# RWKV scans of a two-block model: rows and bonus become a fifth stage, and the order tables of the scan are drawn anew

## The reference, cut to what matters

```python
def rwkv7_scan(r, w, k, v, kk, a):
    def step(state, inp):
        r_t, w_t, k_t, v_t, kk_t, a_t = inp
        sa = jnp.einsum('bhvk,bhk->bhv', state, -kk_t)
        state = (state * w_t[:, :, None, :] + sa[..., None] * (kk_t * a_t)[:, :, None, :]
                 + v_t[..., None] * k_t[:, :, None, :])
        return state, jnp.einsum('bhvk,bhk->bhv', state, r_t)
...
    for d in range(2):      # forward and backward in time
        ...
        o = rwkv7_scan(*ins)
        bonus = jnp.sum(rh * kd * r_k.astype(F32), axis=-1, keepdims=True) * vh
        dir_out.append((group_norm(o, gn_w, gn_b) + bonus.reshape(nB, S, D)) * g.astype(F32))
    y = dir_out[0] + dir_out[1]
    return y.astype(h.dtype) @ w_o
```

## Time and profile before

| | |
|---|---|
| median of 3 runs | 2982.0 us (2981.33 to 2984.5) |
| the profiled execution | 2981.18 us, its span 2979.5 us |
| busy over the span | PE 92%, PEld 73%, DVE 49%, ACT 41%, POOL 14% |
| the scan, from the first products to the end of the last advance | 2077.73 to 2558 us of the span |

### The profile page before, as it was taken

The page is one execution under the profiler, slowest core; times in us unless marked ns, Lnnn a source line. Parts: engine busy times, 40 slices in busy tenths (PEclk is TensorE's granted clock), DMA queues, the critical chain, the costliest instruction groups (busy, mean ns, idle before and its releaser), DMA issues. The chain is left out here.

```text
span 2979.5 us, 56809 instructions
## 1 busy us (share of the span) xinstructions
PE 2738.0 (92%) x24888; PEld 2161.5 (73%) x24888; DVE 1471.0 (49%) x2295; ACT 1214.5 (41%) x2071; POOL 410.2 (14%) x332
## 2 busy tenths in 40 slices
PE   6999999999999999898889999798777877899999
PEld 5877557788878888775578888676666665678887
DVE  2532774743443333526554242985566764453343
ACT  3332564632242222325443232664556654442232
POOL 1001451000000000103100000001444543100000
PEclk9999999999999999999999999899999999899999
DMA  4222002133222222231222222230000001322221
GB/s 160 96 79 85 1 1 92 71 127 113 99 85 99 92 103 95 81 123 67 76 90 99 95 90 99 86 101 31 6 9 8 8 5 36 114 92 100 85 99 71
DMA packets 38821, 228.84 MB, mean 77 GB/s; under 512 B 4352, under 2 KB 8448, under 8 KB 15024
## 3 DMA queue, kind: packets, MB, share of 16 engines
q1 hardware_dynamic: 32576, 201.34, 18.9%
q0 software_dynamic: 6000, 23.87, 2.3%
HBM read 220.93 MB, written 4.26 MB: 76 GB/s over the span
## 5 line engine op out<-in xcount | busy, mean ns | idle before, releaser
L445 DVE TENSOR_TENSOR weights_lo<-ring,weights_hi 128x1024 fp32r<-128x1024 f32 x353 | 435.4, 1236 | 700.6 <-ACT weights_hi L438 700.5
L438 ACT ACTIVATE weights_hi<-ring 128x1024 fp32r<-128x1024 f32 x364 | 382.2, 1053 | 577.7 <-PE bank L575 335.3
L2506 PE MATMUL bank<-scan_low,scan_low 64*64 64x64 f32 x4608 | 106.6, 233 | 53.7 <-DVE scan_low L2910 31.8
L494 PE MATMUL bank<-mlp_h_hi,weights_hi 128*128 128x512 f32 x384 | 151.3, 394 | 2.0 <-DVE mlp_h_lo L790 2.0
L495 PE MATMUL bank<-mlp_h_lo,weights_hi 128*128 128x512 f32 x384 | 151.1, 393 | 0.0
L496 PE MATMUL bank<-mlp_h_hi,weights_lo 128*128 128x512 f32 x384 | 150.7, 392 | 0.0
L494 PE MATMUL bank<-h_hi,weights_hi 128*128 128x512 f32 x384 | 150.1, 391 | 0.0
L573 PE MATMUL bank<-weights_hi,mlp_p_hi 128*128 128x512 f32 x384 | 149.6, 390 | 0.0
L495 PE MATMUL bank<-h_lo,weights_hi 128*128 128x512 f32 x384 | 149.5, 389 | 0.0
L574 PE MATMUL bank<-weights_lo,mlp_p_hi 128*128 128x512 f32 x384 | 149.4, 389 | 0.0
L575 PE MATMUL bank<-weights_hi,mlp_p_lo 128*128 128x512 f32 x384 | 149.4, 389 | 0.0
(11 more groups left out here) (666 smaller groups left out, 6780.3 us busy)
## 6 DMA issues: line engine op xcount, KB each, us to landing
ring<-in_w_m SPq DMA_DIRECT2D x64, 1024.0 KB, 4.5
ring<-in_w_mb SPq DMA_DIRECT2D x24, 1024.0 KB, 4.6
ring<-in_w_fi SPq DMA_DIRECT2D x22, 1024.0 KB, 4.6
ring<-in_w_fo SPq DMA_DIRECT2D x10, 1024.0 KB, 4.8
ring<-in_w_a SPq DMA_DIRECT2D x7, 1024.0 KB, 4.9
attn_bias<-scratch POOLq DMA_DIRECT2D x16, 448.0 KB, 4.6
ring<-in_w_rg SPq DMA_DIRECT2D x5, 1024.0 KB, 4.9
ring<-in_w_v SPq DMA_DIRECT2D x4, 1024.0 KB, 14.4
```

The lines of the kernel that those rows point to most:

```text
L438: act.e.activation(halves(g, s)[0], raw, ACT.Copy).then_inc(*act.up("act_unit_high", ("high", s)))
L445: lane.e.tensor_tensor(lo, raw, hi.bitcast(F32), ALU.subtract).then_inc(*lane.up(f"{lane.name}_unit_low", ("low", s)))
L494: pe.e.matmul(ps[:, :], hi, xh, start=k == 0, stop=False, skip_group_check=True)
L2506: m = pe.e.matmul(out[to], left[rows], right[rows], start=start, stop=stop, skip_group_check=True)
```

## The change

A fifth stage, **rows (r)**, takes `tbk`, `tv`, the bonus and their drains out of the middle, for the same pair as the middle. The middle begins with the products. Steps hold one operation where they held two to four; empty steps and `quanta` are gone; `ORDER` has new strings for all four engines. POOL makes the first level's mask as soon as the first half of DVE's masks is there (`masked_first`), and no longer makes the masks of level 1 directly after each direction's start of the inverse, but after both. The same instructions are issued as before, in another order; the tables of the head of pair 0 (`EARLY`) put its steps at the same places of the phase before.

```diff
-EARLY = 11
+EARLY = {"pe": (0, 1, 1, 1, 2, 3, 3, 3), "act": (1, 1, 2, 3, 5, 8, 8, 12), "dve": (0, 1, 1, 1, 2, 3, 5, 7)}
...
-ORDER = {"pe": "mmmhthathahhmmttamammamahthamattmammamamamamtamamhhamatmtamhtatmhhhtahmamamamththhama",
+ORDER = {"pe": "ramammrahtammammamrmammamtarmamamahhamamamthaamamarmaamammtaaa",
...
-    plan = {"a": (advance, 0), "t": (tail, -1), "h": (head, 2), "m": (middle, 1)}
+    plan = {"a": (advance, 0), "t": (tail, -1), "h": (head, 2), "m": (middle, 1), "r": (rows, 1)}
...
+def pe_rows(g, pe, b):
+
+    R = g.R
     for d in range(2):
 
         banks = [bank(g, pe, ("tbk", b, d, j)) for j in range(2)]
...
+    banks = [bank(g, pe, ("tv", b, j)) for j in range(2)]
...
+    for e in range(2):
+        ps = bank(g, pe, ("bonus", b, e))
...
+def pool_rows(g, pool, b):
+    pool_scaled_eye(g, pool, b, 1)
+    yield
...
+                if e == 0:
+                    dve.mark("masked_first", b, d)
+                yield
...
     for d in range(2):
-        yield
-        if d == 0:
-            pool_scaled_eye(g, pool, b, 1)
-        yield from quanta(2)
         u = slice(8 * d, 8 * d + 8)
-        pool.wait_ge(g.at("masked_products", b, d))
+        pool.wait_ge(g.at("masked_first", b, d))
...
         masked(0, d)
+        yield
         pool.wait_ge(pool.newest)
...
-        masked(1, d)
-    yield from quanta(2)
-    for d in range(2):
-        masked(2, d)
         yield
...
-    for level in range(2, 6):
-        yield
-        for d in range(2) if level < 4 else ():
-            masked(level + 2, d)
-        yield from quanta(2 if level < 5 else 1)
-    yield
+    for level in range(1, 6):
+        for d in range(2):
+            masked(level, d)
+            yield
```

214 lines of the change are left out of this document (94 added, 120 removed).

## The result

The changed kernel takes 2991.02 us (median of 14 runs, 2986.18 to 2996.61), the kernel before 2982.48 in the same batch (14 runs): a ratio of 1.0029, 95% interval 1.0021 to 1.0037. It is 9 us slower where 18 us less was forecast. A difference of 0.001 between two ratios is 3 us. Each ratio has an interval of 0.0008 to 0.0014 to either side, so two ratios must lie 0.001 to 0.002 apart before the difference is clear.

What follows compares the result with a forecast made beforehand. PE, busy 92% of the span, was taken as the bound, with some 10 us idle per full round. Savings of 13 (six full rounds), 4 (fill round) and 1 (round without a head), 18 us, gave 2964 us; range 2947 to 2983.

Steps and rivals of the forecast that it cites:

- y2 to y5: Middle stretch of a full round: the layout gives 25.8 us, including all 1.8 us of stops on code.
- stops on "issue": PE stopping without a semaphore wait, read as 16 KB code blocks arriving; 55.3 us before, to stay near 50.
- the sum of a full round: Products to y2 18.05, y2 to next products 34.0, code stops 1.8: 53.9 us, against 57.3 over all six.
- the opening: Products to y2: 18.05 us instead of 24.85; 4.9 only moved, 1.9 gained by split masks and products first.
- From the end of y5 to the products: End of a round, a DVE chain of 7.0 us behind y5's drain: 8.65 us, where it was 7.15.
- The fill round: First scan round, head and middle alone, 49.01 us before: waits covered by bonus and head matmuls, 4 us less.
- The round without a head: Scan round after the six full ones, 52.17 us before: only y-to-x waits shrink, 1 us less.
- the last advance: End of the scan, a PE and DVE chain over 8 chunks, 35.40 us before: not touched, 0.
- B: Rival: the head's tail, DVE's seven us behind y5, decides; rounds of 58.0 us, 2989 us in all; chance 0.14.
- D: Rival: PE's stall before x0 of the second direction is larger, ACT's copies holding a bank; 2973, within the forecast's 0.50.
- A: Rival: code blocks at 3.5 us decide, y-to-x waits return as stops; only the fill round gains, 2979; chance 0.18.
- C: Rival: stops overlap DVE's lateness and the clock holds; full rounds of 53 us, 2950 in all; chance 0.15.

Runs made afterwards that it cites:

- e9: Changed kernel with four wide matmuls on constants on PE ahead of its wait for POOL before x0 of the second direction: 2987.55 us, ratio 1.0039.
- e2: Changed kernel with the last products step on PE right behind the third and DVE's masks likewise: 2976.33 us, ratio 0.9984.
- e16: Changed kernel with the last products step ahead of kk2 and the variance but behind `tbk` and the advance step, DVE's masks likewise: 2974.50 us, ratio 0.9985.
- e13: Changed kernel with DVE's `kb` ahead of u of chunk 7 and `bonus_in` ahead of the copy of chunk 7: 2983.08 us, ratio 1.0015.
- e14: e2 with DVE's `kb` ahead of u of chunk 7 and `bonus_in` ahead of the copy of chunk 7: 2965.22 us, ratio 0.9956.
- e1: Changed kernel with POOL's last level 5 mask put before its sum of the tail: 2990.03 us, ratio 1.0027.
- e12: e14 with PE's wait for ACT's copies of the output banks behind the first products instead of ahead of them: 2963.18 us, ratio 0.9960.
- e17: e12 with both of DVE's `minus_kk` ahead of `bonus_in`: 2961.10 us, ratio 0.9937.
- e11: e12 with POOL's low part of the tail behind the level 2 masks, and the edit of e1: 2963.06 us, ratio 0.9957.
- e3: Changed kernel with DVE's `bb` ahead of y5's drain, `kb` ahead of u of chunk 7, `bonus_in` ahead of its copy: 2995.53 us, ratio 1.0046.
- e6: e3 with PE's wait for ACT's copies of the output banks behind the first products instead of ahead of them: 2987.79 us, ratio 1.0026.
- e18: e11 with both of DVE's `minus_kk` ahead of `bonus_in`: 2960.03 us, ratio 0.9936.

## Why the prediction was wrong

**What held.** The waits on y's drain were to fall from 31.8 to under 15: 5.2. A stall of 2.5 us on POOL before x0 of the second direction was to appear: 2.39, and eight in all. The products were to wait for `minus_kk` by 1 to 2 us: they begin 0.11 us behind its end, after 2.02 us of idle time. y2 to y5 was to take 25.8 us: 25.9, with some luck. One of its terms, 2.25 us of wait for u of chunk 5, is 0.43 to 0.50 in five full rounds and 1.81 in one. The stops on "issue" were to stay near 50 us and didn't: 40.9 and 2.6 more, of which 7.7 are the waits for `minus_kk`, so some 36 us, where the kernel before had 55.3 and 5.4 more. The Trainium skill's "Runtime: NRT & Kernel Launch", section "Instruction fetch mechanics", calls the cost of a block's edge mostly hidden; with 36 us left the trace still differs, but no result here turned on it.

**The step that failed** is the sum of a full round, 18.05 + 34.0 + 1.8 = 53.9 us. It measured 58.6, with both ends of it laid out too short. A clean round was to take 53 to 55 us; the shortest of the six took 55.6.
- "The last products step has moved behind `tbk`, kk2 and the variance and ends at 8.1; DVE's masks of it (0.41 each, twice) end at 8.9; POOL makes the mask and the start of the second direction (2 x 1.3) until 11.5": 9.65, 11.1 and 13.2 in the round shown. I let the steps of PE follow each other without asking when their banks come free; three waits for DVE's masks, 1.69 us, are not in the layout. (A step has four masks, not two; POOL starts behind the second, so that slip costs it nothing.) Over six rounds this makes x0 1.2 us late.
- "PE does y1, x1 and xt1 with their drains [...], and y2 starts at 18.05": 21.2. Of the 3.1 us, 1.9 lie behind x0. Some 1.0 is the half clock behind the stall (8.3 us from x0 to y2, 7.3 in e9), for which a layout "by hand at the full clock" has no term, and the rest is work of PE that I took too short. So the opening was worth a loss of 1.7 us, not a gain of 1.9: before, it took 24.4, of which 4.9 us only moved, so 19.5 against 21.2. (The 24.85 of the prediction was misread: y2's first records start at 2322.12, so it is 24.4 in that round too, and the gain laid out was 1.5.) e2 and e16 bring it back to 19.2 and 19.3.
- "From the end of y5 to the products this is 8.65 us": 10.0 as the mean of six (9.0 to 10.9). The chain on DVE was named link by link, but with u of chunk 7 and the copy at no wait (1.07 and 0.41) and the two `minus_kk` at 1.37 us (2.35 beside POOL). Moving `kb` gave 4 to 8 us (e13, e14).
- The rounds' mean was to fall by 2.2 us and rose by 1.3: +7.8 us for 13 forecast the other way. The slower clock, which I had said such a round "feels less", was lower in three of them (0.94). My own rows didn't bear out what I made of it: of the rounds before, the one of 58.55 us had 0.97 like the two shortest.

**The fill round** was to get 4 us shorter and got 0.6 (49.01 to 48.43). **The round without a head** was to get 1 shorter and got 1.8 longer; **the last advance**, at a clock of 0.59 for 0.62, got 0.7 longer. 7.8 - 0.6 + 1.8 + 0.7 is the 9.7 us of the scan.

**The rivals.** B, "It decides once the stretch from y5 to the products is over 10.5 us", gave 2989 and had 0.14. The time is near, and one of its reasons holds (long operations slowed beside POOL); but the stretch is 10.0 us as a mean, over 10.5 in two of six rounds only, the sum ahead of the last mask costs nothing (e1), and two thirds of what the layout missed (3.1 of 4.7 us a round) are in the opening, of which B says nothing. Against the kernel before, though, the end grew more (2.7 us a round) than the opening (1.7). D had the right place and nearly the size: "the step comes 1.5 us later and so does all behind it" is what the round shown has (1.55). What held the step was DVE's masks, not ACT's copies, and the stall itself did not grow. A is out, since the stops on "issue" fell where it wanted them to rise by what y's waits lose; C is out by the time.

The order of the changed kernel with two places mended (e12) takes 12 us less than the kernel before. With a third edit, which is no part of the change (e17), it is 18, the forecast's own figure; that is luck. No trace has the 53.9 us of the layout: the shortest mean of six rounds is 54.2 (e11), e12's is 55.1. What is shown is that the new order can be faster than the old one and that two places in it lost that.

**Open.** What the changed kernel would take with the stall filled to the right length; the 1 us a pair for the clock comes from one trace against another. Why moving the wait for the copies gave 6 us beside e3's order (e6), where the products had waited for it (up to 1.07 us behind `minus_kk`), and nothing from e14 to e12, where they had as well (up to 1.06). And where e17's and e18's gain of 6 to 7 us arises.

## What to carry to other kernels

When a layout by hand sums an engine's work in its new order, put down for each step when its output bank is drained and by whom. A step whose bank is late shifts all behind it, and an engine downstream shows it better (POOL idle for 4.52 us) than the one that slid. Ask of each wide operation at the end of a chain what stands between it and the work that it feeds. Where the operation ahead in the queue waits for another engine, putting a wide one before it was worth 4 to 8 us (`kb`); putting another still further ahead, where it waited itself and held up a drain, cost 5 (`bb`). A pass that nobody waits for belongs behind the step that others wait for, where it fills the stall (e16). An edit's sign belongs to the order around it: "products first" gave 13 us in one and took 14 in the other.

## What was not expected of the hardware

The same stall of 2.4 us was followed by a lower clock in six of eight pairs and not in the other two. Two stretches of the changed kernel, each from x0 on, behind a stall of 2.39 and of 2.54 us (columns as in the earlier trace rows):

```profile
2194.06:2199.36 5.30, 5.30 (x204) 5.18 (x206) 2.82 (x6) 3.52 (x6) 5.30 (x5) 1.00 0.01 3
2373.83:2379.13 5.30, 5.30 (x152) 5.30 (x154) 1.53 (x4) 2.51 (x3) 5.12 (x5) 0.68 0.01 3
```

The length of the stall doesn't decide it here: other pairs had 2.38 and 2.39 us of idle time and 0.68 behind it. The first 32 matmuls of these stretches:

```profile
2194.06 1.15 PE L2505 MATMUL bank<-scan_head,scan_low 64*64 64x64 f32 x32 [2.39 <-POOL scan_low L2939]
```

```profile
2373.83 1.92 PE L2505 MATMUL bank<-scan_head,scan_low 64*64 64x64 f32 x32 [2.54 <-POOL scan_low L2939]
```

At the full clock they take 1.15 us, at the half clock 1.92. In e9, where matmuls fill the stall, none of the eight pairs was granted less than 1.00 there. And of DVE's two `minus_kk`, 1.28 us together where they were done before POOL's low part began (e12), the second alone grew where they met it, from 0.68 to 1.75 us, while POOL's operation took 1.74 us instead of 1.27. Both engines lose in such a meeting.
